# Opening with modulation, h and the first three dense rounds in halves, all four modulation units transferred ahead of the halved dense weights

## What is computed

```python
cond = silu(c)
mod = cond @ w_ada[l] + b_ada[l]                     # 1024 x 6144
sh1, sc1, g1, sh2, sc2, g2 = split(mod, 6)
h = rms_norm(x, norm1_gain[l]) * (1.0 + sc1) + sh1
proj = h @ w_in[l]                                   # 1024 x 4864, ten column groups
```

## Time and profile before

| | |
|---|---|
| median of 3 runs | 1562.98 us (1560.12 to 1564.08) |
| span of the profiled execution | 1556.6 us (the page lists no total beside it) |
| PE busy | 1447.0 us, 93% |
| DVE busy | 602.6 us, 39% |
| ACT busy | 342.8 us, 22% |
| DMA | 594.63 MB, 382 GB/s on average |

### The profile page before, as it was taken

One profiled execution on the slowest core, in us unless ns is written; L12 is line 12 of the kernel. 1 busy time (PEld: TensorE's weight loads), 2 busy tenths in 40 slices (PEclk: granted clock), 3 DMA queues, 4 the chain that ended last, 5 costly groups with the idle time before them and its releaser, 6 DMA issues.

```text
span 1556.6 us, 20902 instructions
## 1 busy us (share of the span) xinstructions
PE 1447.0 (93%) x8692; PEld 754.9 (48%) x8692; DVE 602.6 (39%) x920; ACT 342.8 (22%) x395; POOL 22.7 (1%) x36
## 2 busy tenths in 40 slices
PE   5999999999999999999998989999989999998677
PEld 2878985333333333333332333333338999854343
DVE  4686683232223232231321321323247687522111
ACT  4564332010101010110100100101033384321110
POOL 1100100000000000000000000000000000000000
PEclk9999999999999999999999999999999999999889
DMA  9986589999999999999999999999996446999998
GB/s 383 372 324 264 197 351 395 430 428 428 429 427 427 428 429 427 429 427 429 428 428 429 426 427 429 429 427 428 429 403 229 163 163 261 362 386 423 422 422 343
DMA packets 76385, 594.63 MB, mean 382 GB/s; under 512 B 5499, under 2 KB 6753, under 8 KB 36901
## 3 DMA queue, kind: packets, MB, share of 16 engines
q1 hardware_dynamic: 74000, 588.25, 91.5%
q0 software_dynamic: 1792, 4.86, 0.9%
q10 hardware_dynamic: 532, 0.64, 0.1%
HBM read 592.66 MB, written 1.06 MB: 381 GB/s over the span
## 4 chain that ended last, share of the span: by engine, by line
PE 60%; DMA 34%; DVE 3%; issue 1%; SPq 1%; ACT 1%; POOL 0%; DVEq 0%; ACTq 0%
PE PS L563 54%; DMA ring<-in_w_up 26%; DMA ring<-in_w_up_e 6%; PE PS L743 3%; DMA arena<-in_w_in 2%; DMA ring<-in_w_down_e 1%; PE PS L763 1%; PE PS L1528 1%; DVE ring_r L361 1%; DVE arena L853 1%; PE PS L679 1%; SPq L1093 1%; ACT ring_r L356 0%; POOL arena_r L1119 0%; PE PS L1605 0%
## 5 line engine op out<-in xcount | busy, mean ns | idle before, releaser
L563 PE MATMUL PS<-ring,arena 128*64 128x512 f32 x3020 | 671.2, 597 | 41.0 <-DMA ring<-in_w_up 28.7
L563 PEld LDWEIGHTS PS<-ring,arena 128*64 128x64 f32 x3020 | 212.3, 137 | 462.1 <-issue 400.1
L563 PE MATMUL PS<-arena 128*128 128x128 f32 (+12 forms) x1240 | 228.7, 441 | 2.9 <-DVE arena L2109 0.9
L841 DVE TENSOR_SCALAR arena<-PS 128x512 f32<-128x512 f32 x32 | 22.1, 692 | 482.6 <-PE PS L563 482.6
L542 ACT ACTIVATE arena<-arena 128x512 f32<-128x512 f32 x32 | 20.2, 630 | 698.5 <-DVE arena L841 698.5
L563 PE MATMUL PS<-ring_r 128*128 128x256 f32 (+1 forms) x576 | 171.6, 305 | 0.1
L563 PEld LDWEIGHTS PS<-arena 64*128 64x128 f32 (+6 forms) x1240 | 108.6, 164 | 120.4 <-issue 114.9
L563 PE MATMUL PS<-hT_r,ring_r 128*128 128x256 f32 x800 | 151.7, 286 | 0.3 <-DVE ring_r L361 0.3
L361 DVE TENSOR_TENSOR ring_r<-ring,ring_r 128x2048 fp32r<-128x2048 f32 x51 | 116.4, 2291 | 37.2 <-ACT ring_r L356 36.1
L563 PEld LDWEIGHTS PS<-hT_r,ring_r 128*128 128x128 f32 x800 | 127.8, 193 | 2.3 <-issue 1.4
L356 ACT ACTIVATE ring_r<-ring 128x2048 fp32r<-128x2048 f32 x51 | 97.2, 1912 | 104.6 <-PE PS L563 99.2
(11 more groups left out here) (382 smaller groups left out, 965.2 us busy)
## 6 DMA issues: line engine op xcount, KB each, us to landing
ring<-in_w_up SPq DMA_DIRECT2D x128, 2048.0 KB, 20.7
ring<-in_w_down SPq DMA_DIRECT2D x59, 2048.0 KB, 18.6
ring<-in_w_in SPq DMA_DIRECT2D x17, 2048.0 KB, 11.2
ring<-in_w_gate_e SPq DMA_DIRECT2D x14, 2048.0 KB, 19.3
ring<-in_w_down_e SPq DMA_DIRECT2D x13, 2048.0 KB, 20.1
ring<-in_w_up_e SPq DMA_DIRECT2D x13, 2048.0 KB, 19.0
ring<-in_w_ada SPq DMA_DIRECT2D x12, 2048.0 KB, 16.1
ring<-in_w_out SPq DMA_DIRECT2D x4, 2048.0 KB, 7.7
```

The source lines that it names most:

```text
L563: return nc.tensor.matmul(o, w, m, start=first, stop=last)
L841: V.tensor_scalar(glu.rearrange("p (kk b q) -> p kk b q", kk=4, b=2), hu[:, :, :, :, 0], 7.0, None, ALU.min)\
```

## The change

PE's first rows up to the third round are new, and with them the split of h, of the modulation and of in0, in1 and in2 in halves. A half of a round is now rows 0 to 511 or 512 to 1023 of its weights, for all three. A half of the modulation is now columns 0 to 511 or 512 to 1023 of both `sh1` and `sc1`. Units (ada,0,0) and (ada,0,1) hold the first half, the two others the second. They are read by 16 transfers of 512 KB, whose pieces in memory are 512 columns, 2 KB. All 16 stand ahead of the halves of in0, in1 and in2 in SP's list. The buffer of in1 is a new place in the arena, in2 has `ring1`. The first early load of an expert's weights into `ring1` moves behind in7.

`mod_products(2)` and `mod_products(3)`, the second half of the modulation, stand inside in2's first half on PE. The columns are made by a matmul with `mod_sums` (`mod_columns`) instead of a transpose. The reads of the transposed h go through a copy `hN` in SBUF.

The core of the diff:

```diff
-PRE_UNITS = [(("ada", 0, 0), 0), (("ada", 0, 1), 1), (("ada", 0, 2), 2), (("ada", 0, 3), 3), (("in", 0), 9), (("in", 1), 0),
-             (("ada", 1, 0), 1), (("in", 2), 2), (("ada", 1, 1), 3), (("in", 3), 9), (("ada", 1, 2), 1), (("in", 4), 0),
+PRE_UNITS = [(("ada", 0, 0), 0), (("ada", 0, 1), 3), (("in", 0), 9), (("in", 1), 11), (("in", 2), 10), (("ada", 0, 2), 2),
+             (("ada", 0, 3), 1), (("in", 3), 0), (("ada", 1, 0), 3), (("ada", 1, 1), 2), (("in", 4), 1), (("ada", 1, 2), 3),
...
@@ SP
+            def mod_load(m):
+                w = mod_view(m)
+                for c in range(2):
+                    k0 = 4 * (m % 2) + 2 * c
+                    src = t["w_ada"][0, k0 * P:(k0 + 2) * P, 0:2 * D].rearrange("(k p) (s f) -> p k s f", p=P, s=2)
+                    for kk in range(2):
+                        sp.dma_start(w[:, 2 * c + kk, :, :], src[:, kk, :, 512 * (m // 2):512 * (m // 2 + 1)])\
+                            .then_inc(mod_landed(m, c)[0], 16)
...
+            for m in range(4):
+                mod_load(m)
+            for half in range(2):
+                for r in range(OPENING):
+                    opening_half(r, half)
+            sp.dma_start(consts[:, NFIRST:], t["consts"][:, NFIRST:]).then_inc(S("consts"), 16)
+            for u in range(OPENING + 4, len(PRE)):
+                wait(sp, unit_free(before_in_slot(u)))
+                unit_load(sp, u, PRE[u])
...
@@ ACT
+            act.wait_ge(S("h_transposed"), 2)
+            A(*hN_half(0), ACT.Copy).then_inc(S("hN"), 1)
+            split_upper(act, 0)
+            def upper_half(half):
+                act.wait_ge(S("hN"), 2)
+                act.wait_ge(S("modT"), half + 1)
+                for k in range(4 * half, 4 * half + 4):
+                    last = A(hT_up[:, k, :], hN[:, k, :], ACT.Identity, scale=sm("scaleT")[:, k:k + 1],
+                             bias=sm("shiftT")[:, k:k + 1]).then_inc(S("hT_A"), 1)
+            upper_half(0)
+            for n in range(1, OPENING):
+                split_upper(act, n)
             act.wait_ge(S("angles"), 2)
             A(sm("sin"), sm("rr"), ACT.Sin).then_inc(S("sincos"), 1)
             A(sm("cos"), sm("rn"), ACT.Sin).then_inc(S("sincos"), 1)
+            split_upper(act, OPENING)
+            upper_half(1)
+            for n in range(OPENING + 1, 2 * OPENING):
+                split_upper(act, n)
@@ PE
+            def opening_tokens(r, half):
+                n, o = half * OPENING + r, PS[:, banks(r), :]
+                cn = PIECES[n][2].shape[2]
+                ks = slice(4 * half, 4 * half + 4)
+                wu, wl, xu, xl = upper(n), PIECES[n][3], hT_up[:, ks, :], hT_low[:, ks, :]
+                pe.wait_ge(S("w_upper"), n + 1)
+                for m, (a, w) in enumerate(((xu, wu), (xl, wu), (xu, wl))):
+                    if m == 1:
+                        pe.wait_ge(S("hT_lower"), half + 1)
+                    if m == 2:
+                        wait(pe, lower_ready(n))
+                    for k in range(4):
+                        if m == 0:
+                            pe.wait_ge(S("hT_A"), 4 * half + k + 1)
+                        for i in range(TT):
+                            last = mm(o[:, i, 0:cn], a[:, k, i * P:(i + 1) * P], w[:, k, :],
+                                      half == 0 and m == 0 and k == 0, half == 1 and m == 2 and k == 3)
...
-            for n in range(2):
-                ada(n)
+            mod_products(0)
...
             transpose_h(pe, "n1")
-            ada(2)
-            ada(3)
-
-            pe.wait_ge(S("modrow"), 1)
-            for c in range(4):
-                last = nc.tensor.transpose(PS[:, 4, c * P:(c + 1) * P], modrow[:, 0, c * P:(c + 1) * P], ident)
-            last.then_inc(S("rowsT"), 1)
-            keep_warm_short(6, 7)
-            first_tokens()
+            mod_products(1)
+            keep_warm_short(4, 6)
+            mod_columns(0)
+            keep_warm_short(8, 6)
+            opening_tokens(0, 0)
+            pe.wait_ge(S("hN"), 2)
+            opening_tokens(1, 0)
+            opening_cols(2, 0, lambda c: mod_products(2 + c))
+            mod_columns(1)
+            opening_tokens(0, 1)
+            opening_tokens(1, 1)
+            opening_cols(2, 1)
             ada(4)
-            pe.wait_ge(S("hT_V"), 1)
-            split_tokens(1)
-            keep_warm_short(6, 4)
-            split_cols(2)
+            split_cols(3)
             ada(5)
             ada(6)
-            split_cols(3)
@@ DVE
+            def modulated(half):
+                v.wait_ge(S("ada_done"), 2 * half + 2)
+                sig(TV(mod_sums[:, half, :], mod_sums[:, half, :], PS[:, 7, :], ALU.add), "modrow")
+                v.wait_ge(S("rowsT"), half + 3)
...
+                v.wait_ge(S("hN"), 2)
+                for k in range(4 * half, 4 * half + 4):
+                    last = TS(h_full[:, k, :], hN[:, k, :], sm("scaleT")[:, k:k + 1], sm("shiftT")[:, k:k + 1], ALU.mult, ALU.add)
+                L(last)
+                v.wait_ge(S("hT_A"), 4 * half + 4)
+                sig(TV(hT_low[:, c, :], h_full[:, c, :], hT_up[:, c, :], ALU.subtract), "hT_lower")
+
+            modulated(0)
+            for n in range(1, OPENING):
+                split_lower(v, n)
```

More of the change, by code:

```diff
@@ L192, in program, with mod_landed, landings @@
         SLOT_OF = [slot_of(u) for u in range(MOE2 + NSLOT)]
+        MOD_SLOTS = [SLOT_OF[u] for u, d in enumerate(PRE) if d[:2] == ("ada", 0)]
+        def mod_landed(m, c):
+            if m % 2 and c:
+                return S(f"loaded{MOD_SLOTS[m]}"), 32
+            return S(f"loaded{MOD_SLOTS[m - m % 2]}"), 96
+        def landings(s, before):
+            return SLOT_OF[:before].count(s) + 5 * MOD_SLOTS[0::2].count(s) + MOD_SLOTS[1::2].count(s)
         def slot_used(u):
@@ L1234, in _ @@
                 .then_inc(S("big_free_A"), 1)
-            for n in range(3, 5):
-                split_upper(act, n)
             act.wait_ge(S("big_free_A"), 1)
@@ L1289, in _ @@
             A(sm("es"), sm("es"), ACT.Exp).then_inc(S("att_exp"), 1)
-            for n in range(12, 14):
+            for n in range(13, 15):
                 split_upper(act, n)
@@ L1531, in ada, with mod_products @@
                 last.then_inc(S("ada_done"), 1)
+            def mod_products(m):
+                w = mod_view(m)
+                for c in range(2):
+                    wait(pe, mod_landed(m, c))
+                    for s_ in range(2):
+                        for kk in range(2):
+                            k, j = 4 * (m % 2) + 2 * c + kk, 2 * s_ + kk
+                            last = nc.tensor.matmul(PS[32 * j:32 * j + 32, 7, :], sm("cond32")[:, 32 * k:32 * k + 32],
+                                                    w[:, 2 * c + kk, s_, :], start=m % 2 == 0 and c == 0,
+                                                    stop=m % 2 == 1 and c == 1, tile_position=(0, 32 * j))
+                last.then_inc(S("ada_done"), 1)
@@ new lines, in opening_cols @@
+            def opening_cols(r, half, between=None):
+                n, o = half * OPENING + r, PS[:, banks(r), :].rearrange("p b (c t) -> p (b c) t", c=2)
+                ks = slice(4 * half, 4 * half + 4)
+                wu, wl, xu, xl = upper(n), PIECES[n][3], hT_up[:, ks, :], hT_low[:, ks, :]
+                wait(pe, lower_ready(n))
+                for c in range(4):
+                    cs = slice(c * P, (c + 1) * P)
+                    for k in range(4):
+                        for m, (a, w) in enumerate(((xu, wl), (xl, wu), (xu, wu))):
+                            last = mm(o[:, c, :], w[:, k, cs], a[:, k, :],
+                                      half == 0 and c % 2 == 0 and k == 0 and m == 0,
+                                      half == 1 and c % 2 == 1 and k == 3 and m == 2)
+                    if c == 3:
+                        last.then_inc(S("big_done" if half else "half_done"), 1)
+                    elif between and c < 2:
+                        between(c)
```

340 lines of the change are left out of this document (165 added, 175 removed), and 1 row of the table PRE_UNITS.

## The result

The changed kernel takes 1571.3 us (median of 4 runs, 1569.9 to 1573.7). Beside runs of the kernel before on the same chip the ratio is **1.0082, with a 95% interval of 1.0067 to 1.0096**: 0.82% slower, some 12.8 us. The forecast of 1569.6 was a ratio of 1.0042 and its range, 1567.5 to 1572, one of 1.0029 to 1.0058. The median of 1571.3 lies in that range only because the range was counted from 1562.98; the ratio lies above it. The direction was right and so was most of the mechanism. Of the size, 6.6 of 12.8 us were forecast.

The account below looks back on a forecast made before the run. PE's opening was taken to bound the kernel, with everything from the experts on fixed relative to it. PE 6.4 us late, +6.6 us with DVE, gave a span of 1563.2 and a time of 1569.6 us (+0.42%), range 1567.5 to 1572.

Parts of the forecast that it names:

- Steps 1 and 2: Opening: 2 KB pieces delay in0's first half by 1.9 us, ACT's split starts at 31.1, PE starts at 33.5.
- Step 3: in0's first half, 24 products: 5.7 us plus 2.45 for PE's slow clock after a long pause, ending at 41.65.
- Step 4: in1's and in2's first halves with two modulation units inside in2's, the units costing 3.7 us in full; end 54.0.
- Step 5: Turn to the second half: columns, scale, shift and one activation take 1.2 us; waits of 2.2 us are not hidden.
- Step 6: Rest of the opening: in3 ends at 84.0, two `ada` at 87.6, against 81.24 before, so PE is 6.4 us late.
- Step 7: DVE's chain behind in1 shrinks from 28.6 to 24.5 us; total delay taken as +6.6 us; ACT has 2 in hand for in5.
- rival B: DVE and ACT become the bound: chain does not shrink or in5 comes late; 4 us more, 1573; chance 0.10.
- the prediction's own sign: Wrong if the first experts' start moves by less than 4 us or more than 10, or moves without the end.
- A: Small pieces and the clock cost nothing: sum 3.2 us instead of 6.6, time 1566.2; chance 0.20.
- C: The experts absorb the loss: their 428 GB/s stream starts as before and the time stays at 1563; chance 0.07.
- D: in0's half overtakes the two later modulation units in the queue, PE starts 10.9 us earlier, time 1557; chance 0.05.

Follow-up runs that it names:

- e5: Changed kernel with modulation units loaded as 8 transfers of 8 KB pieces instead of 16 of 2 KB (modulation values wrong, only times count); ratio 1.0062 to the kernel before.
- e4: Changed kernel with transfers interleaved: two modulation units, three first halves, two modulation units, three second halves; ratio 1.0034 to the kernel before.
- e1: Changed kernel with 36 short warming matmuls instead of 8 ahead of in0's first half; ratio 1.0069 to the kernel before.
- e6: Changed kernel with both e1's 36 warming matmuls and e2's lower part on DVE; ratio 1.0068 to the kernel before.
- e2: Changed kernel with the lower part of in0's first half made by DVE instead of POOL; ratio 1.0079 to the kernel before.
- e13: e2 with POOL's two small loads of the q and k gains held until ACT's first split; ratio 1.0051 to the kernel before.
- e3: Changed kernel with the third and fourth modulation units multiplied ahead of in0 instead of inside in2's first half; ratio 1.0055 to the kernel before.
- e11: Changed kernel with the second half's modulation columns ahead of the last quarter of in2's first half; ratio 1.0047 to the kernel before.
- a0_changed: The changed kernel run and profiled again, nothing altered; ratio 1.0079 to the kernel before.
- e8: Changed kernel with e4's transfer order and e2's lower part on DVE; ratio 1.0015 to the kernel before.
- e9: Changed kernel with in5 loaded into in2's buffer and the early expert load there issued later; ratio 1.0068 to the kernel before.
- e10: e8 (transfer order, lower part on DVE) with e9's buffer for in5 added; ratio 1.0008 to the kernel before.
- e12: Changed kernel with four edits: transfer order, lower part on DVE, in5's buffer, columns ahead of in2's last quarter; ratio 0.9999 to the kernel before.
- e14: e12 with POOL's two small loads held until ACT's first split; median 1556.85 us, ratio 0.9984 to the kernel before.

## Why the prediction was right in direction and wrong in size

**Steps 1 and 2 held.** Split at 31.1 forecast, 30.98 measured; PE at 33.5 and 33.52. e5 and the rates beside it show that the 1.8 us are the pieces' price.

**Step 3 failed in DVE's price.** The step took "half of 2.92", 1.46, for DVE's subtraction. It measured 3.65, and DVE was done at 38.6 and not at 36.4. The row of 2.92 us was itself no free one: POOL's operation ran from 31.16 for 4.56 us, to 35.7, and DVE started at 34.94. A subtraction of the same width takes 2.29 in the earlier trace rows. 0.8 of waiting and 2.29 give 3.1, close to 2.92. In the changed kernel DVE starts 2.56 ahead of POOL's end, and 2.56 + 1.23 is 3.8, close to 3.65. DVE does not slow down; it stands until POOL is done. The Trainium skill (SBUF — State Buffer, SBUF: two separate sides) says this: the two engines share a port pair as "an exclusive lock, not a bandwidth split", taken by DVE operations in a two-port mode, or with two SBUF inputs if POOL's operation reads SBUF. The rows agree, with 3.65 against 1.23 here and one scaling of 4.31 among three of 0.40 in e4. I had halved a duration that held a constant. The slow first group was forecast too, but over-priced: 2.45 from another place, and 1.6 measured (3.75 for 2.12). So the half ended at 42.5, only 0.9 later than the forecast 41.65; by luck one error covered most of the other. In the changed kernel the slow clock was worth nothing, because DVE's wait hid it (e1). With that wait gone it is worth about 1 us: the 24 products take 7.2 us at full clock (e6), 8.0 and 8.3 with the slow start (e2, e13).

**Step 4 held.** 12.35 us forecast, 12.4 measured; e3 gives 2.7 to 3.3 of its 3.7 back.

**Step 5 failed by 1.0 us.** Columns were taken as 0.4 and measured 0.95. From the last product to the first it took 2.3 us for 1.3. e11 gives it back.

**Step 6 was 1.1 us short.** It had no second fall of the clock. From the second half's first product to the `ada` ahead of in3 it took 15.8 us, for 15.35 in the forecast and 15.1 in a0_changed, where the clock didn't fall. The fall isn't certain: at the same turn a0_changed, e1, e2, e8, e9 and e13 ran their first eight products at full pace (2.1 us), e3, e4, e5 and e6 slow (2.9 to 3.3), with equal waits. And in3 took 12.15 us, in a0_changed and e11 as well, where the forecast had 11.52. 0.2 of that is a wait for its last lower part; the rest isn't explained.

So in3 ended at 87.0 and not at 84.0: 0.9 from step 3, 1.0 from step 5, 1.1 from step 6. PE was 9.4 us late at the end of the three `ada`, not 6.4.

**Step 7** had the chain of DVE in balance, which held (PE waited 0.21 us for it), and in5 with "about 2 us in hand". It had none, not even by the step's own numbers: an issue at 84 and some 8 us more make 92, and ACT wanted it at 91. ACT waited 2.96, and 0.5 to 0.7 came through (e9). That is rival B in kind, at a seventh of its price.

**The rest of the difference.** At the experts the profile shows +10.0 where I had +6.6. The ratio stands for 12.8. By the prediction's own sign it is wrong if the experts' start moves by more than 10 us; it moved by 10.0, and by 11.1 in a0_changed. Of the last 2.8 us, 1.4 is the one slow stretch in this profile; e4, e10, e12, e13 and e14 have it too, the others don't. At 140 to 160 us the granted clock reads from 0.83 to 1.00, up to 3.4 us, and 0.91 in the kernel before. Whether the changed kernel has more such falls over many runs isn't shown, so the cause of the last 2.8 us stays open. The carried distance of 6.4 us between median and profiled execution was a bad base as well: spans lie 1.8 to 1.9 below their own run's time, and the kernel before ran at a median of 1558.7 beside a0_changed. It hid part of the error in the absolute time.

**Rivals.** A (pieces and clock free) is refuted for the pieces by e5, and for the clock it was right by another mechanism: the cost was covered. C is refuted: 10 us at the gates were 10 at the experts. D did not happen by itself, and e4 made it by hand. There it brought PE's start forward by 6.4 us, not 10.9.

## What to carry to other kernels

When a transfer list is cut finer, its order is worth more than its cuts: ask which piece the first waiting engine needs, since moving two modulation units from ahead of it to behind it brought 6 us. Before a duration of DVE is scaled to another size, look what POOL did at the time. When an engine is freed of a wait, look what it will issue sooner. Put short serial steps between two halves under the end of the first half, so that PE has no pause.

## What the hardware showed that I had not expected

- Two equal 128x1024 subtractions on DVE took 3.65 and 1.23 us; the longer one overlapped a POOL subtraction and ended 1.1 us behind it. Four scalings from SBUF beside POOL took 5.28 for 1.38, one of them 4.31 and the others 0.40 each (e4); in the kernel before, whose scalings read PSUM, they took 1.90 with POOL running.
- Two 32 KB loads from POOL's queue, 64 packets, took 5.9% of the 16 DMA engines over 25 us, with a hole of 153 GB/s between 7 and 9 us, and a 1 MB transfer landed 1.6 us later (e2, e13).
- A wait of 3.01 us behind a full-pace group was followed by a granted clock of 0.79 in the next 8 us (e1), and at the turn a wait of 1.17 us was followed by slow products in one profile of the changed kernel (3.09 us for eight) and by full pace in the other (2.12).
- Modulation weights in 2 KB pieces moved at 387 GB/s and in 8 KB pieces at 420 (e5), the DMA engines full in both.
